# A fused NSA and differential-attention layer: turning the second attention's probabilities on VectorE, scaling the first attention's on ScalarE

## What is computed

```
h    = rms_norm(x);  proj = h @ w_in                 # 2048 x 7704 columns, cut into q, k, v, gates z
# first attention (NSA), 8 heads in 2 groups; branches: compressed, selected, window
p    = softmax(mask(q @ k.T * scale))                # per head and branch
o_a  = gate[..., 0] * o_cmp + gate[..., 1] * (p_sel @ v_s) + gate[..., 2] * (p_win @ v_w)
# second attention (differential), 4 heads, two softmax maps each
a    = p[:, 0] - lam * p[:, 1]                       # 256 x 256 per head
o_b  = rms_norm(a @ v) * (1 - lambda_init)
out  = rms_norm(x + concat(o_a * silu(z_a), o_b * silu(z_b)) @ w_out)
```

## Time and profile before

| | |
|---|---|
| median of 3 runs | 497.95 us (497.92 to 498.12) |
| profiled execution, its own time | 498.4 us |
| its span, first to last instruction | 496.1 us |
| mean granted TensorE clock | 0.994 |
| TensorE busy (products) | 483.1 us, 97% |
| VectorE busy | 357.6 us, 72% |
| ScalarE busy | 218.9 us, 44% |
| GpSimd busy | 44.2 us, 9% |

### The profile page before, as it was taken

One profiled execution on the slowest core, in us unless ns is written; L12 is line 12 of the kernel. 1 busy time (PEld: TensorE's weight loads), 2 busy tenths in 40 slices (PEclk: granted clock), 3 DMA queues, 4 the chain that ended last, 5 costly groups with the idle time before them and its releaser, 6 DMA issues.

```text
span 496.1 us, 6302 instructions
## 1 busy us (share of the span) xinstructions
PE 483.1 (97%) x2462; PEld 391.8 (79%) x2462; DVE 357.6 (72%) x497; ACT 218.9 (44%) x296; POOL 44.2 (9%) x41
## 2 busy tenths in 40 slices
PE   6999999999999999999999999999999999999993
PEld 5788867777777888888888888888888888888882
DVE  3865979358495888999898848488897998454542
ACT  4847414334332454444345554564535443434331
POOL 1003400020100102010020000002000000203030
PEclk9999999999999999999999999999999999999997
DMA  7999857876789433435254335525784554665005
GB/s 258 411 420 419 347 198 304 314 318 260 329 336 360 161 159 102 153 118 221 86 180 155 122 138 180 170 100 209 279 345 169 169 176 189 245 219 190 0 3 167
DMA packets 17868, 107.70 MB, mean 217 GB/s; under 512 B 2224, under 2 KB 2736, under 8 KB 5936
## 3 DMA queue, kind: packets, MB, share of 16 engines
q1 hardware_dynamic: 16544, 104.86, 56.1%
q10 hardware_dynamic: 1296, 2.44, 1.3%
HBM read 105.20 MB, written 2.10 MB: 216 GB/s over the span
## 4 chain that ended last, share of the span: by engine, by line
PE 94%; issue 2%; DMA 2%; SPq 1%; DVE 1%; ACT 0%; POOLq 0%; POOL 0%; DVEq 0%
PE acc L1022 26%; PE acc L1024 25%; PE acc L1023 25%; PE S L1162 3%; PE O L1063 3%; DMA raw<-stream 2%; PE S L1179 1%; PE acc L1046 1%; PE acc L1048 1%; PE acc L1047 1%; PE S L1024 1%; PE S L1023 1%; PE S L1022 1%; PE O L1203 1%; PE O L1198 1%
## 5 line engine op out<-in xcount | busy, mean ns | idle before, releaser
L662 DVE TENSOR_TENSOR wlo<-raw,whi 128x2048 fp32r<-128x2048 f32 x72 | 165.7, 2304 | 85.8 <-ACT whi L412 84.9
L412 ACT ACTIVATE whi<-raw 128x2048 fp32r<-128x2048 f32 x72 | 137.9, 1917 | 169.9 <-PE acc L1024 156.8
L1022 PE MATMUL acc<-whi,hT_hi 128*128 128x512 f32 x432 | 171.6, 397 | 0.0
L1023 PE MATMUL acc<-wlo,hT_hi 128*128 128x512 f32 x432 | 168.4, 390 | 0.0
L1024 PE MATMUL acc<-whi,hT_lo 128*128 128x512 f32 x432 | 168.3, 390 | 0.0
L1022 PEld LDWEIGHTS acc<-whi,hT_hi 128*128 128x128 f32 x432 | 81.1, 188 | 23.1 <-issue 6.7
L1024 PEld LDWEIGHTS acc<-whi,hT_lo 128*128 128x128 f32 x432 | 81.1, 188 | 17.3
L1023 PEld LDWEIGHTS acc<-wlo,hT_hi 128*128 128x128 f32 x432 | 81.2, 188 | 16.2
L374 POOL TENSOR_TENSOR stage<-stage,stage 128x512 f32<-128x512 f32 (+1 forms) x16 | 23.4, 1480 | 184.8 <-DVE stage L708 184.8
L488 ACT ACTIVATE e<-S,small 128x128 f32<-128x128 f32 (+1 forms) x48 | 19.6, 420 | 26.1 <-DVE small L754 26.1
L717 DVE STREAM_TRANSPOSE zT<-stage 32x256 f32<-32x256 f32 x64 | 27.9, 436 | 1.9
(11 more groups left out here) (156 smaller groups left out, 499.6 us busy)
## 6 DMA issues: line engine op xcount, KB each, us to landing
raw<-stream SPq DMA_DIRECT2D x72, 1024.0 KB, 4.9
row_raw<-stream SPq DMA_DIRECT2D x16, 1024.0 KB, 6.3
raw<-stream SPq DMA_DIRECT2D x6, 512.0 KB, 10.7
x_nat<-x_rows SPq DMA_DIRECT2D x2, 1024.0 KB, 13.3
x_nat<-x_rows SPq DMA_DIRECT2D x1, 2048.0 KB, 7.8
result<-x_nat SPq DMA_DIRECT2D x8, 256.0 KB, 3.2
xTs<-xT SPq DMA_DIRECT2D x3, 512.0 KB, 9.6
raw<-stream SPq DMA_DIRECT2D x4, 256.0 KB, 6.5
```

Source lines behind the costliest of these rows:

```text
L412: act.activation(whi[:, n % SPLIT, :], raw[:, n % RAW, :], ACT.Copy).then_inc(hi_ready, 1)
L662: dve.tensor_tensor(wlo[:, n % SPLIT, :], raw[:, n % RAW, :], whi[:, n % SPLIT, :].bitcast(f32), ALU.subtract)\
L1022: pe.matmul(acc_bank(n), xh, wh, start=k == 0, stop=False)
L1023: pe.matmul(acc_bank(n), xh, wl, start=False, stop=False)
```

## The change

In the first attention `weights` now only makes the coefficients; the 8 scalings are done by ScalarE (`scale_probs`) in step U + 2, behind ScalarE's split, with a new semaphore `coef_ready`. In the second attention TensorE no longer turns the probabilities. VectorE does it in step U + 3 (`turn_probs_b`): for each of the 4 by 4 pairs of 32-row strips, one transpose of 32x2x32 from `e0` and one of 32x2x2x32 from `e1`, into `pTf`, which lies in the half of `pT` that the second attention leaves unused. `take_pT` and `take_pT_lo` then read `pTf` in SBUF and not `S` in PSUM; ScalarE waits until all 32 transposes of the unit are done (`pb_turned`).

```diff
--- before.py
+++ after.py
@@ -180,6 +180,7 @@
         gwf = sb("gwf", [P, KT, N_GATE], at=r_e)
         gw = sb("gw", [P, KT, 32], at=r_e + 4 * KT * N_GATE)
         pT = sb("pT_hi", [P, 3, NB], f32r, at=r_p)
+        pTf = sb("pTf", [P, 3, NB], at=r_p)[:, :, NB // 2:NB]
         junk = sb("junk", [P, 2, NB], at=r_p)
         kvcT = sb("kvcT", [P, 4, SEQ], at=r_p)
         zT = [sb("zT0", [P, 4, SEQ], at=r1), sb("zT1", [P, 4, SEQ], at=r1 + 4096)] + [sb("zT2", [P, 4, SEQ], at=r_e)] * 2
@@ -248,6 +249,7 @@
         lam_sums, lam_exp = sem("lam_sums"), sem("lam_exp")
         scores_done, max_ready, exp_done, probs_ready = (
             sem(n) for n in ("scores_done", "max_ready", "exp_done", "probs_ready"))
+        coef_ready, pb_turned = sem("coef_ready"), sem("pb_turned")
         probs_turned, pT_hi_ready, pT_lo_ready, pv_done, o_taken = (
             sem(n) for n in ("probs_turned", "pT_hi_ready", "pT_lo_ready", "pv_done", "o_taken"))
         cs_done, cs_masked, cs_shift, ce_done, pc_ready, pc_turned, pcT_ready = (
@@ -489,13 +491,25 @@
                                        bias=nmax[:, 4 * t + i:4 * t + i + 1],
                                        accum_out=sums[:, 4 * t + i:4 * t + i + 1]).then_inc(exp_done, 1)
 
+            def scale_probs(u):
+                act.wait_ge(coef_ready, u + 1)
+                for t in range(TT):
+                    e = e0 if t == 0 else e1
+                    for i in range(4):
+                        act.activation(e[:, i, :], e[:, i, :], ACT.Copy, scale=coef[:, 4 * t + i:4 * t + i + 1])\
+                            .then_inc(probs_ready, 1)
+
             def take_pT(u):
-                w = NB if u < N_A else NB // 2
+                a = u < N_A
                 if u:
                     act.wait_ge(pv_done, TT * u)
+                if not a:
+                    act.wait_ge(pb_turned, SQ * (u - N_A + 1))
                 for k in range(3):
-                    act.wait_ge(probs_turned, 3 * u + k + 1)
-                    act.activation(pT[:, k, 0:w], S[:, k, 0:w], ACT.Copy).then_inc(pT_hi_ready, 1)
+                    if a:
+                        act.wait_ge(probs_turned, 3 * u + k + 1)
+                    src = S[:, k, :] if a else pTf[:, k, :]
+                    act.activation(pT[:, k, 0:NB if a else NB // 2], src, ACT.Copy).then_inc(pT_hi_ready, 1)
 
             def take_oa(g):
                 for t in range(TT):
@@ -618,6 +632,9 @@
                 for u in range(N_UNITS):
                     if c == UNIT_AT[u] + 1:
                         exps(u)
+                for u in range(N_A):
+                    if c == UNIT_AT[u] + 2:
+                        scale_probs(u)
                 if c == UNIT_AT[1] + 5:
                     take_oa(0)
                 if c == UNIT_AT[3] + 5:
@@ -766,12 +783,14 @@
                     .then_inc(acc_read["v"], 1)
 
             def take_pT_lo(u):
-                w = NB if u < N_A else NB // 2
+                a = u < N_A
                 if u:
                     dve.wait_ge(pv_done, TT * u)
                 for k in range(3):
+                    w = NB if a else NB // 2
+                    src = S[:, k, :] if a else pTf[:, k, :]
                     dve.wait_ge(pT_hi_ready, 3 * u + k + 1)
-                    dve.tensor_tensor(pT_lo[:, k, 0:w], S[:, k, 0:w], pT[:, k, 0:w].bitcast(f32), ALU.subtract)\
+                    dve.tensor_tensor(pT_lo[:, k, 0:w], src, pT[:, k, 0:w].bitcast(f32), ALU.subtract)\
                         .then_inc(pT_lo_ready, 1)
 
             def weights(u):
@@ -779,14 +798,11 @@
                 g, br = unit_a(u)
                 dve.wait_ge(exp_done, 8 * (u + 1))
                 link(dve.reciprocal(coef, sums))
-                link(dve.tensor_tensor(coef.rearrange("p (t h) -> p t h", t=TT), coef.rearrange("p (t h) -> p t h", t=TT),
-                                       gate[:, :, :].rearrange("p t (h b) -> p t h b", b=3)[:, :, 4 * g:4 * g + 4, br],
-                                       ALU.mult))
-                for t in range(TT):
-                    e = e0 if t == 0 else e1
-                    for i in range(4):
-                        dve.tensor_scalar(e[:, i, :], e[:, i, :], coef[:, 4 * t + i:4 * t + i + 1], None, ALU.mult)\
-                            .then_inc(probs_ready, 1)
+                if u:
+                    dve.wait_ge(probs_ready, 8 * u)
+                dve.tensor_tensor(coef.rearrange("p (t h) -> p t h", t=TT), coef.rearrange("p (t h) -> p t h", t=TT),
+                                  gate[:, :, :].rearrange("p t (h b) -> p t h b", b=3)[:, :, 4 * g:4 * g + 4, br],
+                                  ALU.mult).then_inc(coef_ready, 1)
 
             def weights_b(u):
 
@@ -802,6 +818,20 @@
                     for i in range(2):
                         dve.scalar_tensor_tensor(e[:, i, :], e[:, i, :], coef[:, 4 * t + i:4 * t + i + 1], e[:, 2 + i, :],
                                                  ALU.mult, ALU.add).then_inc(probs_ready, 1)
+
+            def turn_probs_b(u):
+
+                dve.wait_ge(pv_done, TT * u)
+                dve.wait_ge(probs_ready, 8 * N_A + 4 * (u - N_A + 1))
+                f1 = e1[:, 0:2, :].rearrange("p h (n k) -> p n h k", n=TT)
+                d0 = pTf[:, 0, :].rearrange("p (h q) -> p h q", h=2)
+                d1 = pTf[:, 1:3, :].rearrange("p n (h q) -> p n h q", h=2)
+                for i in range(4):
+                    ri = slice(SQ * i, SQ * (i + 1))
+                    for j in range(4):
+                        rj = slice(SQ * j, SQ * (j + 1))
+                        dve.transpose(d0[rj, :, ri], e0[ri, 0:2, rj]).then_inc(pb_turned, 1)
+                        dve.transpose(d1[rj, :, :, ri], f1[ri, :, :, rj]).then_inc(pb_turned, 1)
 
             def take_ob(u):
 
@@ -952,6 +982,8 @@
                         maxes(u)
                     if c == UNIT_AT[u] + 2:
                         (weights if u < N_A else weights_b)(u)
+                    if u >= N_A and c == UNIT_AT[u] + 3:
+                        turn_probs_b(u)
                 for u in range(N_A, N_UNITS):
                     if c == UNIT_AT[u] + 5:
                         take_ob(u)
@@ -1164,18 +1196,16 @@
                 shared["units"] = u + 1
 
             def turn_probs(u):
-                a = u < N_A
+
                 banks_free()
                 if u == 0:
                     pe.wait_ge(cs_masked, TT)
                 if u == 1:
                     pe.wait_ge(pcT_ready, 1)
-                before = sum(8 if v < N_A else 4 for v in range(u))
                 for k, (t, kt) in enumerate(((0, 0), (1, 0), (1, 1))):
-                    n = 4 if a else 2
-                    pe.wait_ge(probs_ready, before + n * (t + 1))
+                    pe.wait_ge(probs_ready, 8 * u + 4 * (t + 1))
                     e = e0 if t == 0 else e1
-                    for i in range(n):
+                    for i in range(4):
                         last = pe.transpose(S[:, k, i * P:(i + 1) * P], e[:, i, kt * P:(kt + 1) * P], ident)
                     last.then_inc(probs_turned, 1)
                 shared["pT"] = u + 1
@@ -1250,7 +1280,7 @@
                 if c == CMP_SCORES_AT + 4:
                     turn_cmp()
                 for u in range(N_UNITS):
-                    if c == UNIT_AT[u] + 3:
+                    if c == UNIT_AT[u] + 3 and u < N_A:
                         turn_probs(u)
                     if c == UNIT_AT[u] + 4:
                         (pv_a if u < N_A else pv_b)(u)
```

## The result

| | before | after |
|---|---|---|
| median of the runs (us) | 498.00 (497.92 to 498.12) | 508.56 (508.13 to 508.94) |
| profiled execution (us) | 498.4 | 508.13 |
| its span (us) | 496.1 | 506.0 |
| mean granted clock of TensorE | 0.994 | 0.988 |

The change makes the kernel **slower by 2.1%**: ratio 1.0211, 95% interval 1.0198 to 1.0225, or +10.6 us on the medians. The interval lies wholly above 1, so the kernel is slower; whether by more than 2% it leaves open.

The account below looks back on a forecast made before the run. TensorE, busy 483.1 of 496.1 us, was taken to bound the kernel. Net stall costs of 5.9 and 4.9 us plus 3.0 us for the clock gave +13.8 us on a median of 497.95: 511.7 us, range 502 to 516.

Parts of the forecast that it names:

- Turns off TensorE: Second attention, units 4 and 5: TensorE loses 6 turns per unit, 0.66 us each unit, -1.3 us in all.
- ScalarE's scaling: First attention, units 0 to 3: ScalarE's 8 scalings per unit are hidden, nothing taken; upper bound 0.3 us late in unit 1.
- T: Time of VectorE's 32 turns in each of units 4 and 5: 9.5 us, bounds 5.6 and 14.9 us.
- The stalls: TensorE stands 6.5 us at chunk 60's second half in unit 4, 5.5 us before unit 5's PV products.
- The clock: Behind both stalls TensorE runs at half speed for a while: +3.0 us, bounds 0 and 3.7 us.
- VectorE's backlog: After unit 5 VectorE is 4.7 us further behind TensorE; priced at nothing, 0.5 us left in the range.
- Sum: Net stall costs 5.9 and 4.9 us plus 3.0 us for the clock: +13.8 us, profiled execution 498.4 to 512.2 us.
- the first: Same stalls in units 4 and 5, less cost: full clock 508.7 us, or turns of 5.6 us 500.8 us; chance 0.26.
- The second: Units 4 and 5: turns hidden if under 3.0 us per unit, kernel faster at 496.6 us; chance 0.04, shared with another rival.

Follow-up runs that it names:

- the earlier turns: Changed kernel with VectorE's weights and turns of units 4 and 5 a chunk earlier, unit 4's `vb_lo` ahead of the split: 496.69 us.
- The single squares: Changed kernel with every VectorE turn cut into 32x32 pieces, 96 calls per unit instead of 32: 516.55 us, one run.
- the filled gaps: Changed kernel with 16 unused filler products ahead of chunk 60's second half and 12 ahead of unit 5's PV: 506.03 us.
- the turns alone: Kernel before with only VectorE's turning of the second attention's probabilities added, first attention's scaling left on VectorE: 508.68 us, ratio 1.0216.
- `vb_lo` ahead of the turns: Changed kernel with VectorE's reading of block 10's first token tile put ahead of unit 4's turns: 506.78 us, ratio 1.0173.

## Why the prediction was right, and which term was off

The forecast, 511.7 us (502 to 516), had the sign, the range and the mechanism right. The centre was 3.1 us high. Its steps, one by one:

- **Turns off TensorE**, -1.3 us: the trace has -0.69 twice, -1.4. Confirmed; only with the earlier turns does it show at the end of the kernel (-1.55 us on the medians).
- **ScalarE's scaling**, nothing, at most 0.3 us: nothing, by three comparisons. Its upper bound was above the truth although one scaling takes longer (391 and 494 ns) than the exponentials that I bounded it by the earlier trace rows: the bound adds durations, and successive scalings overlap, 2.88 us for eight against 3.54 by their durations.
- **T**, 9.5 us: 7.38. **This is the mis-sized term.** The step took the fixed part per call, 0.20 us, and the slope, 1.02 ns per element, from rows of another operation (TENSOR_TENSOR) and asked only that they meet the one turn known, at 256 elements. The single squares measured 0.06 us and 1.8 ns for turns of 32 to 128 elements. The two mixtures come out close at 256 elements (0.46 and 0.51 us; measured 0.467) and part for the small ones, 0.33 and 0.29 us at 128, 0.27 and 0.17 at 64. The bounds, 5.6 and 14.9, held it.
- **The stalls**, 6.5 and 5.5 us: 4.54 and 3.54. Each is about 2.0 us too long, and T was 2.1 us too long. The room (3.0 us), the bank that holds chunk 60, and the chain through `pT` in unit 5 were right: with T = 7.4 the same working gives 4.4 and 3.4.
- **The clock**, +3.0 us: 1.68 + 1.59 = 3.27. That the fall is the gaps' doing was inferred from the ends of the program and is now shown, by the filled gaps (clock 1.00 throughout, 3.07 us back). That the size came so near is in part luck. Its own two figures of 1.85 us would have made 3.7, and they rest on the 314 ns of the warming products alone, since the granted clock reads 1.00 there too (2.0 to 5.5 us). The 3.0 was a choice between bounds of 0 and 3.7, and the loss is not the same in every execution. In the profile of the turns alone, with the same gaps, it is 2.27 + 1.58 = 3.85 us. The forecast had cited the Trainium skill, TensorE: Matmul & The Clock Gate, section on the HAM clock gate, for what it calls the default state; a gap in the middle, which no row of before could show, behaves the same way.
- **VectorE's backlog**, nothing: right for this kernel. With the gaps filled and TensorE at full speed two waits of 0.8 us in all come up.
- **Sum** of the profiled execution: +13.8 forecast, +9.9 in the spans. The two stalls take off 3.9, the entry at chunk 60 takes off 0.15, the turns 0.1, and the clock adds 0.3. That is the difference.

Of the rivals, the first (same stalls, less cost) had put T at 9.5 with no loss of clock, or at 5.6: the truth has a T between and the full loss of clock, so neither. The second (turns hidden) had to have 0.09 us per turn; it is 0.23. But my argument against it was wrong in one point: I read off the 32x256 turn that turns don't overlap. A turn of 64 elements lasts 0.236 us, and its successor starts 0.17 us after it. Small ones overlap, and still cost too much. The price per 128x128 square of the Trainium skill, VectorE: DVE Perf Modes, section The three transpose paths, gave as an estimate 1.9 us per unit, from bf16. Measured here, fp32 in 32 calls: 7.38. The trace doesn't agree with that estimate for this form; no run has a bf16 turn, so the page's own figure is not tested here.

Left open: whether all three moves of the last version are needed (only the whole was run), and what the clock does after gaps between 1.39 and 2.6 us. Behind the one of 1.39 us, in the changed kernel's prologue (ahead of the product at 9.90), the products are soon spaced 0.23 us as at full speed; after each gap of 2.6 us or more there was a fall.

## What to carry to other kernels

Work given to an engine that is 72% busy is not free for that: it is free only if it fits between the last thing that engine did for TensorE and the next thing that TensorE needs from it. Here that was 3.0 us at one place, and one reading of two timelines gave it. Work that doesn't fit there should be moved to where its inputs are ready, a step earlier here, and then the removed TensorE time does come off the end. When an operation's price at a new size is wanted, two sizes of that operation are needed; a line through another operation's rows can meet the one known size and miss all others.

## What was not expected of the hardware

- **Small turns on VectorE.** Pitch from one start to the next: 0.117 us for 32x32 (11.23 / 96), 0.17 for 32x64, 0.29 for 32x128, 0.467 for 32x256. The durations in the rows are 0.16 to 0.18, 0.236, 0.260 and 0.436 us, so up to 64 elements successive turns overlap, and beyond that there is a short gap. A duration alone misleads in both directions.
- **Scaling on ScalarE is slower than on VectorE**, 391 and 494 ns against 281 and 346 ns for 128x128 and 128x256 (the latter two are the same scalings on VectorE in the kernel before). Eight of them take 2.88 us on ScalarE.
- **When the clock falls differs from gap to gap, and so does the price.** In the changed kernel TensorE idled for 4.4 us, and the stretch from 311 to 312 still reads 1.00. The three products behind the gap are spaced 0.30, 0.35 and 0.42 us, then 0.43 (the low level, 1.2 GHz), until 315.66. With the turns alone the same gap, 4.36 us long, has the fall inside it (stretches of TensorE's time, then the product that ends the gap):

```profile
309.00:310.00 1.00, 0.00 (x0) 0.84 0.00 0
310.00:311.00 1.00, 0.00 (x0) 0.50 0.00 0
...
311.85 0.77 PE L1054 MATMUL acc<-whi,hT_hi 128*128 128x512 f32 x1 [4.36 <-DVE vb_lo L779]
```

TensorE had done nothing for 2.2 us when it fell, near 309.7, and the half behind the gap takes 4.99 us (311.85 to 316.84) instead of 2.72, 2.3 us more and not 1.7. After the shorter gap of 2.6 us (`vb_lo` ahead of the turns) the fall came 0.9 us after the restart, in the midst of full work. At the end of the program it comes with no restart at all, 2.5 to 3 us after the last product. So a gap's price is not in the gap: it is in the work behind it, 1.5 to 2.3 us for the gaps of 2.6 to 4.4 us here, and 2.7 and 1.8 us for the two of 8.2 and 7.1 us (single squares). Why the moment of the fall differs, no run here shows.
